# All weights laid out on the host in load order, one 8 KB row per partition and transfer

## What is computed

```python
# first block: three mixers
x = x + (o * silu(gate)) @ w_out            # o from h @ w_in, h = rms_norm(x)
...
def swiglu(h, w_gate, w_up, w_down):         # w_gate, w_up: 1024 x 3584; w_down: 3584 x 1024
    return (jax.nn.silu(h @ w_gate) * (h @ w_up)) @ w_down
...
def recurrent_mixer(h, w_in, conv_w, conv_b, ga_w, ga_b, gx_w, gx_b, lam, w_out):
    y_branch, x_branch = jnp.split(h @ w_in, 2, axis=-1)
    ...
    r = jax.nn.sigmoid(jnp.einsum('bshi,hij->bshj', xh, ga_w).reshape(B, S, LRU_WIDTH) + ga_b)
    i = jax.nn.sigmoid(jnp.einsum('bshi,hij->bshj', xh, gx_w).reshape(B, S, LRU_WIDTH) + gx_b)
...
    def expert_block(args):                  # moe: tokens of one expert, for each of 8
        tok, e = args
        xb = xf[tok]
        hb = jax.nn.silu(xb @ w_gate[e]) * (xb @ w_up[e])
        return hb @ w_down[e]
```

## Time and profile before

| | |
|---|---|
| median of three runs | 2190.58 us (2189.98 to 2190.78) |
| the profiled execution | 2191.68 us, its span 2189.9 us |
| TensorE / VectorE / ScalarE busy | 92% / 73% / 56% of the span |
| moved by DMA | 499.97 MB in 235489 packets |
| q1 (SyncE) | 498.61 MB, 64.2% of 16 DMA engines over the span |
| mean granted clock of TensorE | 0.958 |

### The profile page before, as it was taken

How to read it: one execution, slowest core, us unless ns; L and a number is a source line. 1 busy time by engine, 2 the same in 40 slices (tenths; PEclk the granted TensorE clock), 3 DMA queues, 4 the chain that set the end, 5 groups by cost and what they waited for, 6 DMA issues and landing times.

```text
span 2189.9 us, 26599 instructions
## 1 busy us (share of the span) xinstructions
PE 2006.3 (92%) x9492; PEld 1669.4 (76%) x9492; DVE 1593.0 (73%) x1965; ACT 1228.1 (56%) x1475; POOL 150.8 (7%) x222
## 2 busy tenths in 40 slices
PE   5998989688987799999858999999999999999998
PEld 4776877567767678887847887888888888888886
DVE  4673985557665744454765889888888989888887
ACT  3552034535553344343444776777777777777775
POOL 3203401305011000000000000000000000000000
PEclk9999999799998789999977999999999999999999
DMA  7531333214414226555233999999999999999995
GB/s 258 169 101 45 123 135 113 90 58 154 163 40 163 96 89 200 182 184 191 97 118 117 379 343 337 376 334 373 333 376 345 361 367 342 376 333 372 335 372 189
DMA packets 235489, 499.97 MB, mean 228 GB/s; under 512 B 9294, under 2 KB 41042, under 8 KB 235274
## 3 DMA queue, kind: packets, MB, share of 16 engines
q1 hardware_dynamic: 235312, 498.61, 64.2%
q10 hardware_dynamic: 90, 0.23, 0.0%
HBM read 497.75 MB, written 1.05 MB: 228 GB/s over the span
## 4 chain that ended last, share of the span: by engine, by line
PE 80%; DVE 10%; ACT 5%; issue 2%; POOL 1%; DMA 1%; ACTq 0%; DVEq 0%; POOLq 0%
PE psum L842 23%; PE psum L844 22%; PE psum L843 22%; PE psum L1848 4%; DVE low L827 3%; ACT high L824 2%; PE psum L2769 2%; PE psum L2830 1%; PE psum L1856 1%; POOL small L1081 1%; DMA arena<-in_rg_lambda 1%; ACT h L1580 1%; PE psum L1097 1%; DVE x L1182 1%; PE psum L1864 0%
## 5 line engine op out<-in xcount | busy, mean ns | idle before, releaser
L827 DVE TENSOR_TENSOR low<-raw,high 128x2048 fp32r<-128x2048 f32 (+2 forms) x461 | 1048.8, 2280 | 336.3 <-ACT high L824 332.1
L824 ACT ACTIVATE high<-raw 128x2048 fp32r<-128x2048 f32 (+2 forms) x461 | 878.7, 1911 | 444.8 <-PE psum L844 421.6
L842 PE MATMUL psum<-high,yT_high 128*128 128x512 f32 x1672 | 670.2, 401 | 72.1 <-issue 32.1
L844 PE MATMUL psum<-high,yT_low 128*128 128x512 f32 x1672 | 658.9, 394 | 0.0
L843 PE MATMUL psum<-low,yT_high 128*128 128x512 f32 x1672 | 658.9, 394 | 0.0
L842 PEld LDWEIGHTS psum<-high,yT_high 128*128 128x128 f32 x1672 | 319.3, 191 | 147.3 <-issue 57.5
L844 PEld LDWEIGHTS psum<-high,yT_low 128*128 128x128 f32 x1672 | 319.6, 191 | 68.0
L843 PEld LDWEIGHTS psum<-low,yT_high 128*128 128x128 f32 x1672 | 320.1, 191 | 61.8
L842 PE MATMUL psum<-high,hT_high 128*128 128x512 f32 (+2 forms) x560 | 221.8, 396 | 22.4 <-DVE low L827 12.0
L844 PE MATMUL psum<-high,hT_low 128*128 128x512 f32 (+2 forms) x560 | 217.8, 389 | 0.0
L843 PE MATMUL psum<-low,hT_high 128*128 128x512 f32 (+2 forms) x560 | 217.5, 388 | 0.0
(11 more groups left out here) (322 smaller groups left out, 1788.0 us busy)
## 6 DMA issues: line engine op xcount, KB each, us to landing
raw<-in_moe_w_gate SPq DMA_DIRECT2D x112, 1024.0 KB, 5.4
raw<-in_moe_w_up SPq DMA_DIRECT2D x112, 1024.0 KB, 5.5
raw<-in_moe_w_down SPq DMA_DIRECT2D x112, 1024.0 KB, 5.0
raw<-in_a_w_in SPq DMA_DIRECT2D x32, 1024.0 KB, 5.8
raw<-in_ffn_w_gate SPq DMA_DIRECT2D x14, 1024.0 KB, 5.1
raw<-in_ffn_w_up SPq DMA_DIRECT2D x14, 1024.0 KB, 5.1
raw<-in_ffn_w_down SPq DMA_DIRECT2D x14, 1024.0 KB, 4.8
raw<-in_b_w_in SPq DMA_DIRECT2D x12, 1024.0 KB, 5.1
```

What stands on the lines that cost most here:

```text
L824: eng.activation(high, raw, ACT.Copy).then_inc(k.high_ready, 1)
L827: eng.tensor_tensor(low, raw, high.bitcast(F32), ALU.subtract).then_inc(k.low_ready, 1)
L842: pe.matmul(out, lhs.high, rhs.high, start=start, stop=False)
L844: return pe.matmul(out, lhs.low, rhs.high, start=False, stop=stop)
```

## The change

On the host, every granule is now copied into an array in the order of the loads, `weights[g]` of 128 x 2048 floats, with each partition's blocks side by side (`packed`); the eight experts' granules go to `moe_weights[expert, i]` in the same way. In the kernel a load reads the first c*n floats of each of the 128 rows. The two gate matrices of r become one granule with one DMA, and TensorE's second wait there (`gates_ready`) is gone. The order of loads, the buffers, every wait for a buffer, the small loads and all arithmetic are as before; on TensorE, VectorE, ScalarE and GpSimd the same instructions stand in the same order.

```diff
+def packed(a):
+
+    c, n = a.shape[0] // P, a.shape[1]
+    return a.reshape(c, P, n).transpose(1, 0, 2).reshape(P, c * n)
...
     def rows(a, c0, c1, col, n):
-        return a[P * c0:P * c1, col:col + n].rearrange("(c p) n -> p c n", p=P)
+        return packed(a[P * c0:P * c1, col:col + n])
...
-                        src = w["ffn_w_down_2"][0][row:row + 2 * P, :].rearrange("(c p) n -> p c n", p=P)
+                        src = packed(w["ffn_w_down_2"][0][row:row + 2 * P, :])
...
                 if kind == "gates" and i == 0:
-                    granules.append(Granule(None, None, (layer, "gates", R_HEADS - 1), banks.order[(layer, "gates", R_HEADS - 1)], True))
+                    gates = [packed(w[f"rg_gate_{g}_w_2"][0].reshape(R_HEADS * P, P)) for g in "ax"]
+                    granules.append(Granule(np.concatenate(gates, axis=1), (2 * R_HEADS, P), (layer, "gates", R_HEADS - 1),
+                                            banks.order[(layer, "gates", R_HEADS - 1)], True))
...
-        if granule.src is None:
-
-            dst = k.raw[:, g % RAW, :].rearrange("p (g h n) -> p g h n", g=2, h=R_HEADS)
-            sp.dma_start(dst[:, 1], k.w["rg_gate_x_w_2"][0].rearrange("h p n -> p h n")).then_inc(k.gates_ready, 16)
-            sp.dma_start(dst[:, 0], k.w["rg_gate_a_w_2"][0].rearrange("h p n -> p h n")).then_inc(k.landed[g % RAW], 16)
-            continue
         c, n = granule.shape
-        dst = k.raw[:, g % RAW, 0:c * n].rearrange("p (c n) -> p c n", c=c)
-        sp.dma_start(dst, granule.src).then_inc(k.landed[g % RAW], 16)
+        sp.dma_start(k.raw[:, g % RAW, 0:c * n], k.w["weights"][g][:, 0:c * n]).then_inc(k.landed[g % RAW], 16)
...
             if i == 0:
                 k.wait_landed(pe, g)
-                pe.wait_ge(k.gates_ready, 16)
...
-        a = k.w[f"moe_w_{kind}_2"][0][bass.ds(expert, 1)].rearrange("e a b -> (e a) b")
-        if kind == "down":
-            row = FF_STEP * j + 2 * P * half
-            src, c = a[row:row + 2 * P, :], 2
-        else:
-            src, c = a[4 * P * half:4 * P * (half + 1), FF_STEP * j:FF_STEP * (j + 1)], 4
-        dst = k.raw[:, slot, :].rearrange("p (c n) -> p c n", c=c)
-        sp.dma_start(dst, src.rearrange("(c p) n -> p c n", p=P)).then_inc(k.landed[slot], 16)
+        src = k.w["moe_weights"][bass.ds(expert, 1), i].rearrange("e p n -> (e p) n")
+        sp.dma_start(k.raw[:, slot, :], src).then_inc(k.landed[slot], 16)
...
+def pack_weights(granules):
+
+    weights = np.zeros((len(granules), P, GRANULE), np.float32)
+    for g, granule in enumerate(granules):
+        weights[g, :, 0:granule.src.shape[1]] = granule.src
+    return weights
```

More of the change, by code:

```diff
@@ L536, with __init__ @@
 class Core:
-    def __init__(self, nc, ctx, w, consts, const_at, out):
+    def __init__(self, nc, ctx, w, consts, const_at, out, banks, plan):
         self.nc, self.w, self.consts, self.out = nc, w, consts, out
-        self.banks = plan_banks()
-        self.granules, self.first_granule, self.halves = plan_granules(w, self.banks)
+        self.banks = banks
+        self.granules, self.first_granule, self.halves = plan
         self.engine_steps = {}
@@ L655, in __init__ @@
         self.out_rstd_ready = sem("out_rstd_ready")
-        self.gates_ready = sem("gates_ready")
         self.c_low_staged = sem("c_low_staged")
@@ L3044, with build @@
 LAYERS = ("a0", "b", "c", "a1", "h", "ffn", "r", "moe")
-def build(nc, w, consts, const_at, out, layers=LAYERS):
+def build(nc, w, consts, const_at, out, banks, plan, layers=LAYERS):
     with ExitStack() as ctx:
-        k = Core(nc, ctx, w, consts, const_at, out)
+        k = Core(nc, ctx, w, consts, const_at, out, banks, plan)
         block = ctx.enter_context(nc.Block())
@@ L3119, in store, with pack_experts @@
     sp.wait_ge(k.stored, 16)
[L3122 to L3126, removed]
+INPUTS = tuple(VECTOR_ROWS) + tuple(SPREAD) + ("x", "moe_router_2")
+WEIGHTS = ("a_w_in", "a_w_out", "b_w_in", "b_w_out", "c_w_in", "c_w_uq", "c_w_ukv", "c_w_out", "hy_w_in_2", "hy_w_out_2",
+           "rg_w_in_2", "rg_gate_a_w_2", "rg_gate_x_w_2", "rg_w_out_2", "ffn_w_gate_2", "ffn_w_up_2", "ffn_w_down_2")
+def pack_weights(granules):
[3 more added lines that the diff above has]
+    return weights
+def pack_experts(gate, up, down):
+    weights = np.zeros((N_EXPERTS, ROUND, P, GRANULE), np.float32)
+    for e in range(N_EXPERTS):
+        for i, (kind, j, half, _, _) in enumerate(ROUND_GRANULES):
+            if kind == "down":
+                row = FF_STEP * j + 2 * P * half
+                block = down[0, e, row:row + 2 * P, :]
+            else:
+                block = {"gate": gate, "up": up}[kind][0, e, 4 * P * half:4 * P * (half + 1), FF_STEP * j:FF_STEP * (j + 1)]
+            weights[e, i] = packed(block)
+    return weights
 def kernel(**inputs):
@@ L3138 @@
         w[name] = nc.dram_tensor(f"in_{name}", a.shape, mybir.dt.from_np(a.dtype), kind="ExternalInput").ap()
+    banks = plan_banks()
+    plan = plan_granules({name: np.asarray(inputs[name]) for name in WEIGHTS}, banks)
+    packs = {"weights": pack_weights(plan[0]),
+             "moe_weights": pack_experts(*(np.asarray(inputs[f"moe_w_{kind}_2"]) for kind in ("gate", "up", "down")))}
+    for name, a in packs.items():
+        arrays[f"in_{name}"] = a
+        w[name] = nc.dram_tensor(f"in_{name}", a.shape, F32, kind="ExternalInput").ap()
     consts, const_at = constants()
@@ L3142 @@
     out = nc.dram_tensor("out_x", (1, SEQ, D), F32, kind="ExternalOutput").ap()
-    build(nc, w, const_ap, const_at, out)
+    build(nc, w, const_ap, const_at, out, banks, plan)
     results = run_bass_kernel_spmd(nc, [arrays], core_ids=[0])
```

## The result

| | before | after |
|---|---|---|
| median, 9 runs each | 2190.78 us | 2197.82 us (2195.57 to 2201.55) |
| ratio | | 1.003, 95% interval 1.002 to 1.0039 |
| span of the profiled execution | 2189.9 us | 2196.7 us |
| packets | 235489 | 71762 |

The account below looks back on a forecast made before the run. TensorE was taken to bound the kernel, with one DMA wait in the chain, at the start. Its landing 5.3 us later, other terms nothing, gave 2190.58 + 5.3 = 2195.9 us; range 2189.8 to 2198.0, leaving out C, D and little else.

Parts of the forecast that it names:

- What bounds the kernel: Whole span: TensorE sets the expert stage, loads wait for buffers; the chain's one DMA is in the first 21 us.
- Price of an 8 KB packet: Weight loads: 329 ns each, from c_w_ukv's transfer, against 362 ns for four 2 KB packets; worth nothing in the expert stage.
- rival D: Expert stage: 8 KB packets read memory worse than 2 KB ones; at 380 ns +24 us, 2215; chance 0.04.
- Issue and gates: SyncE's issue of loads, and the two gate loads made one with one TensorE wait less: each worth 0.
- The turn: Start, shared DMA engine: each vector row waits for one 8 KB packet, 329 ns instead of 141; landing 5.3 us later.
- The spacing: q10 from 10 to 14 us: packets near 490 ns apart, 8 of them instead of 13.
- rival A: Shared engine at the start divides bytes, not packets; time the same, 2190.1 us; chance 0.30 together with E.
- SyncE's first four issues: Start: SP issues the first four granules in 2 us instead of 9.8.
- Nothing absorbs the shift: After the first product at 30.02 us the chain is TensorE and engines waiting for it, so all 5.3 us remain.
- E: Weight loads: transfers are cut again to 2 KB pieces, nothing changes, 2190.6 us; chance 0.30 together with rival A.
- B: Start: q10's packets also start earlier, saving half of the delay; +2.6 us, 2193.2; chance 0.09.
- Rival C: Start: small loads overtake; at most some 4 to 5 us faster, 2186 us; chance 0.06.

Follow-up runs that it names:

- first_four_2k: The changed kernel with the first four granules read as four runs of 2 KB per partition again: 2191.57 us, ratio 1.0001 to before.
- the four packet sizes: First four granules in packets of 1, 2, 4 KB (changed kernel) and 8 KB (kernel before): 2190.43, 2191.57, 2196.20, 2198.58 us.
- one-part kernel: The kernel before with only the first four granules loaded in rows of 8 KB: 2198.58 us, ratio 1.0030 to before.
- rows_one_8k: The changed kernel with the 19 vector loads replaced by one DMA of 64 rows packed on the host: 2186.22 us, ratio 0.9976 to before.
- small_first_8k: The changed kernel with one vector load, and the spread loads and router issued ahead of the first weights: 2190.64 us, ratio 0.9996 to before.
- rows_one_2k: The kernel before with the 19 vector loads replaced by one DMA of 64 rows packed on the host: 2186.28 us, ratio 0.9979.
- small_packed_8k: The changed kernel with vectors, spread loads and router packed on the host, issued ahead of the first weights: 2185.18 us, ratio 0.9971 to before.

## Why the prediction was right, point by point

- **What bounds the kernel.** Right. All granules but the first four were not on the path; `first_four_2k` (1.0001) shows it for the 470 others together, in both signs.
- **Price of an 8 KB packet, 329 ns from one transfer.** Good enough: the queue's row of 1860 to 1960 us gives 0.918 x 16 x 100 us / 4295 large packets (4839 less 544 small) = 342 ns, 4% more. The slower rival D (a bound at 371 ns) had no case.
- **Issue and gates.** Nothing shows that they are worth anything: `first_four_2k`, which has the new form of both, is at 1.0001.
- **The turn.** Right as a mechanism, shown by the four packet sizes and by the steps between q10's packets. As a size: landing forecast at 26.2, measured 27.0 (27.5 in the one-part kernel), and 1.3 us of that (1.7 us there) is the one slow packet, which the prediction did not have. Without it the rows would have landed at some 25.7 and 25.9 us (an estimate: the landing less what the packet took over its usual 46 or 159 ns). So the turns were priced 0.3 to 0.5 us too high, and the slow packet was missing from the sum.
- **The spacing.** Forecast near 490 ns, and 8 packets of q10 from 10 to 14 us. The rows of the first load stood 490 ns apart in the median, as forecast; the count was 15, because small loads and completions of other engines fall into that stretch, and a count for all engines could not tell the forecast from rival A.
- **SyncE's first four issues** at 2 us: right. That it would run ahead freely was half right; it was held up again at the sixth spread load.
- **"Nothing absorbs the shift."** Right: 6.1 us at the first product, 6.8 at the end.
- **Rival A** (bytes, or whole DMAs) was the one given most room, 0.30, together with E. The small difference that I had against it, equal numbers of packets rather than equal bytes, pointed the right way. By the Trainium skill's account (DMA: Bandwidth & Descriptors, Queues, rings and completion order) an engine drains a packet of some 9 to 17 descriptors from one queue before it turns to the next. The step of one descriptor of q1 per turn, at all four sizes, disagrees, and the measurement decides. The prediction also read too much out of that account when it let a DMA's whole share of an engine pass in one turn: before the change that share was 32 descriptors.
- **Rivals B and E.** B, that half of the delay is saved by earlier starts (+2.6 us), falls: the first product came 6.1 us later, and 4.8 us of that without the slow packet. E, that 8 KB packets are cut to 2 KB, falls with q1's 212 packets for 1.58 MB from 10 to 14 us, where there were 719 for 1.44 MB.
- **Rival C** was priced at "at most some 4 to 5 us" from the end of x's transposes. Once the vectors were out of the way the first product came 5.6 to 6.0 us earlier. In the two profiled executions the whole span was 7.0 and 5.4 us shorter (2182.9 and 2184.5 against 2189.9), in the medians 4.5 and 4.4. Executions of `rows_one_8k` differ among themselves by 3.4 us, so no separate cause can be read out of the difference.

The sum came to 2195.9 us against 2197.8: forecast +5.3, measured +7.0.

## What to carry to other kernels

Look at what shares a DMA engine with a stream before making the stream's packets larger. Here a small load on another queue got one packet in per packet of the stream, so its latency grew with their size even though the stream became cheaper. The load of 31 rows and the loads of one row went through one engine. Packed into one load of 64 rows they left the path, and the size of the stream's packets made no difference that these runs could tell from none. Where a queue is 97% busy but its issuer waits for buffers, cheaper transfers bring nothing.

## What the runs showed of the hardware that I had not expected

- Between 10 and 18 us of `small_first_8k`, eleven loads that broadcast a row to 128 partitions and one of 32-byte pieces kept q1 occupied, with the engines 12 to 20% busy in every 2 us step; packed on the host, the same data left the engines at 1.02. From 14 to 16 us only broadcast rows of 512 bytes went (238 of them, at a share of 0.20), so the low share is not the 32-byte pieces' alone. Whether the form of the broadcasts or the number of DMAs costs this was not tried.
- Packets of 4 KB already cost most of what 8 KB do: the landing moved by 4.6 us from 2 to 4 KB, and by 1.6 to 2.1 us from 4 to 8, each with its slow packet. The prediction's count fits that: in 68 turns all four granules pass the engine at either size, as 64 packets of 165 ns (10.6 us) or 32 of 329 ns (10.5 us).
- Cutting a load of 31 rows into 16 and 15 brought its queue's last landing forward by 5.8 us, though there was one DMA more.
- In every kernel TensorE starts slowly behind the pause before the first product: matmuls of 512 columns start 0.43 us apart, and then 0.23 us apart. The change comes 5.1 us behind the first product in the kernel before, 3.7 in `rows_one_8k`, 5.5 in `rows_one_2k` and 5.9 in `small_packed_8k`. At the first product the granted clock reads 1.00 in the first two and 0.50 in the last two, so go by the matmuls' spacing. Why the change comes earlier or later is not shown. The chains of `rows_one_8k` and `small_packed_8k` where it comes:

```profile
26.88 0.43 PE psum L844
...
28.51 0.24 PE psum L843
```

```profile
28.66 0.43 PE psum L843
...
30.33 0.23 PE psum L844
```
